# Weight splits of the mixer in halves, and two of the attention output's splits at the end of their slot

## The reference

```python
h = rms_norm(x, norm_mix_g); proj = h @ w_in
ca, cg, q, k, v, iq, ik, iw, z, xbc, dt = split(proj)
u = silu(layer_norm(causal_dwconv31(ca * sigmoid(cg))))      # group A
att = sparse_attention(rms_norm(q), rms_norm(k), v, iq, ik, iw, rel_bias)  # top 128 keys a query
y = ssd_scan(silu(causal_dwconv4(xbc)), softplus(dt + dt_bias), ...)       # Mamba-2, chunks of 128
y = rms_norm((y + d_skip * xs) * silu(z))
x = x + concat([u, att, y]) @ w_out
h = rms_norm(x, norm_ffn_g)
fa, fg = split(causal_dwconv3(h @ w_up))
x = x + (silu(fg) * fa) @ w_down
```

## Time and profile before

| | us |
|---|---|
| median of 3 runs | 713.55 (713.54 to 713.59) |
| profiled execution, its own time | 713.43 |
| span of that profile | 711.7 |
| busy: PE, DVE, ACT, POOL | 694.2, 547.5, 380.7, 140.5 |
| w_lo whole, DVE line 644 | 24 x 2.32, 7.9 idle before them |
| w_hi whole, ACT line 938 | 24 x 1.91, 3.6 idle before them |

### The profile page before, as it was taken

How to read it: one execution, slowest core, us unless ns; L and a number is a source line. 1 busy time by engine, 2 the same in 40 slices (tenths; PEclk the granted TensorE clock), 3 DMA queues, 4 the chain that set the end, 5 groups by cost and what they waited for, 6 DMA issues and landing times.

```text
span 711.7 us, 9787 instructions
## 1 busy us (share of the span) xinstructions
PE 694.2 (98%) x3402; PEld 558.0 (78%) x3402; DVE 547.5 (77%) x852; ACT 380.7 (53%) x570; POOL 140.5 (20%) x114
## 2 busy tenths in 40 slices
PE   4999999999999999999999999999999999999998
PEld 3776888767676788788898888888888888888886
DVE  4368979987899958677668687886766776997995
ACT  6354655989878775533463444344243333654660
POOL 2000477844465302233400000000000000000000
PEclk9999999999999999999999999999999999999999
DMA  8731314112121243312326578766688647864442
GB/s 247 225 138 61 119 59 119 60 60 83 36 62 58 62 177 104 103 60 61 89 90 175 182 205 250 217 170 188 183 244 250 188 154 293 294 221 146 164 163 88
DMA packets 87555, 104.10 MB, mean 146 GB/s; under 512 B 6872, under 2 KB 65592, under 8 KB 87520
## 3 DMA queue, kind: packets, MB, share of 16 engines
q1 hardware_dynamic: 87375, 103.12, 46.2%
q10 hardware_dynamic: 144, 0.52, 0.2%
...
## 4 chain that ended last, share of the span: by engine, by line
PE 79%; DVE 10%; ACT 6%; issue 2%; POOL 2%; DMA 1%; DVEq 0%; ACTq 0%; POOLq 0%
PE bank L1771 70%; DVE u_acc L626 3%; PE bank L1777 3%; DVE w_lo L644 2%; DVE xbcT L1431 2%; PE bank L1791 2%; ACT w_hi L938 1%; POOL u_acc L864 1%; PE bank L2035 1%; DVE prob L1410 1%; PE bank L1930 1%; DMA x_in<-in_x 1%; PE bank L1979 1%; ACT prob L1056 1%; PE bank L1955 1%
## 5 line engine op out<-in xcount | busy, mean ns | idle before, releaser
L1771 PE MATMUL bank<-h_hi,w_hi 128*128 128x512 f32 (+1 forms) x496 | 192.7, 389 | 0.0
L1771 PE MATMUL bank<-h_hi,w_lo 128*128 128x512 f32 (+1 forms) x496 | 189.9, 383 | 0.0
L1771 PE MATMUL bank<-h_lo,w_hi 128*128 128x512 f32 (+1 forms) x496 | 189.8, 383 | 0.0
L1625 DVE SCALAR_TENSOR_TENSOR f<-bank,prm,f 128x511 f32<-128x511 f32 x88 | 65.8, 747 | 60.9 <-ACT f L1186 55.4
L1771 PEld LDWEIGHTS bank<-h_hi,w_hi 128*128 128x128 f32 x496 | 93.3, 188 | 19.6 <-issue 2.1
L1771 PEld LDWEIGHTS bank<-h_hi,w_lo 128*128 128x128 f32 x496 | 93.2, 188 | 18.6
L1771 PEld LDWEIGHTS bank<-h_lo,w_hi 128*128 128x128 f32 x496 | 93.3, 188 | 17.4
L864 POOL TENSOR_TENSOR u_acc<-tapped,u_acc 128x511 f32<-128x511 f32 (+29 forms) x60 | 89.0, 1483 | 44.3 <-ACT tapped L1133 41.0
L1186 ACT ACTIVATE f<-bank,prm 128x512 f32<-128x512 f32 x44 | 34.2, 777 | 70.6 <-PE bank L1771 70.4
L644 DVE TENSOR_TENSOR w_lo<-w_raw,w_hi 128x2048 fp32r<-128x2048 f32 x24 | 55.7, 2320 | 8.0 <-ACT w_hi L938 7.9
L626 DVE SCALAR_TENSOR_TENSOR u_acc<-u_in,prm,u_acc 128x511 f32<-128x511 f32 (+29 forms) x60 | 53.3, 901 | 0.9
...
## 6 DMA issues: line engine op xcount, KB each, us to landing
...
```

What stands on the lines that cost most here:

```text
L1625: ins = dve.scalar_tensor_tensor(out=fbuf[:, 2 * s + v, i:], in0=bank[FFN_BANK[2 * s + v]][:, 0:SEQ - i], scalar=prm[:, bass.ds(tile + (R_ ...
L1771: ins = pe.matmul(o, a, b, start=first and i == 0 and q == 0, stop=last and i == n - 1 and q == 2)
```

## The change

It splits each mixer chunk's high and low part in two halves of 1024 columns. The first half of the high part stays in slot 4c - 4 and its second half goes to 4c - 3; the first half of the low part stays where the whole one was and the second goes to slot 4c - 2. Chunk 23 has all four in slot 4c - 4; chunk 18 has both low halves in 4c - 2. New semaphores `w_hi_half` and `w_lo_half` count first halves; `w_hi_ready` and `w_lo_ready` count second halves, so that PE, SP and the reuse of slots wait for the whole chunk as before. `attout` of blocks 1 and 2 moves from `front` to `fill`. Code for a share of the low part on POOL, which was unused (`POOL_LO` was empty), is removed. The order of instructions on PE, POOL and SP is the same as before.

```diff
@@ make_plan
     for c in range(1, UP0 + 1):
-        fill[4 * c - 4].append(("hi", c))
-        fill[4 * c - (2 if c == LATE_LO else 3 if c < UP0 else 4)].append(("lo", c))
+        one = 0 if c == UP0 else 1
+        fill[4 * c - 4].append(("hi", c, 0))
+        fill[4 * c - 4 + one].append(("hi", c, 1))
+        fill[4 * c - (2 if c == LATE_LO else 4 - one)].append(("lo", c, 0))
+        fill[4 * c - 4 + 2 * one].append(("lo", c, 1))
...
         if hp == NPAIR - 1:
-            front[n + 1].append(("attout", b))
+            (fill if b in (1, 2) else front)[n + 1].append(("attout", b))
@@ PLAN
-        ("norm", 3), ("hTev", 0), ("hTev", 1), ("hi", 0), ("hTev", 2), ("hTev", 3), ("hTlo", 0),
-        ("hTlo", 1), ("hTlo", 2), ("hTlo", 3), ("lo", 0), ("wsplit",)] + make_plan()
+        ("norm", 3), ("hTev", 0), ("hTev", 1), ("hi", 0, 0), ("hi", 0, 1), ("hTev", 2), ("hTev", 3), ("hTlo", 0),
+        ("hTlo", 1), ("hTlo", 2), ("hTlo", 3), ("lo", 0, 0), ("lo", 0, 1), ("wsplit",)] + make_plan()
@@ SP
-                if s[0] == "lo" and s[1] + NSLOT < UP0 + 2:
+                if s[0] == "lo" and s[2] == 1 and s[1] + NSLOT < UP0 + 2:
                     load(s[1] + NSLOT)
@@ ACT
-            def split_hi(c):
-                act.wait_ge(w_landed[c % NSLOT], 32 * (c // NSLOT + 1))
-                if c >= NSLOT:
-                    act.wait_ge(acc_step, STEP[("chunk", c - NSLOT)])
-                act.activation(whi[:, c % NSLOT, :], wraw[:, c % NSLOT, :], ACT.Copy)\
-                    .then_inc(w_hi_ready, 1)
+            def split_hi(c, n):
+                if n == 0:
+                    act.wait_ge(w_landed[c % NSLOT], 32 * (c // NSLOT + 1))
+                    if c >= NSLOT:
+                        act.wait_ge(acc_step, STEP[("chunk", c - NSLOT)])
+                act.activation(whi[:, c % NSLOT, half_cols(n)], wraw[:, c % NSLOT, half_cols(n)], ACT.Copy)\
+                    .then_inc(w_hi_ready if n else w_hi_half, 1)
@@ DVE
                 elif k == "lo":
-                    part_lo(dve, s[1], w_lo_ready)
+                    _, c, n = s
+                    dve.wait_ge(w_hi_ready if n else w_hi_half, c + 1)
+                    w = (slice(None), c % NSLOT, half_cols(n))
+                    dve.tensor_tensor(wlo[w], wraw[w], whi[w].bitcast(F32), ALU.subtract)\
+                        .then_inc(w_lo_ready if n else w_lo_half, 1)
```

More of the change, by code:

```diff
@@ L92 @@
 DW_POOL = (1, 2)
-POOL_COLS = 640
-POOL_LO = []
 def turn_banks(b):
@@ L636, in width, with half_cols @@
             return 2048 if p < NP2 else 1536
[L638 to L645 removed]
+        def half_cols(n):
+            return slice(1024 * n, 1024 * n + 1024)
         @block.sync
@@ L865, in _ @@
                                            u_acc[:, j, i:], ALU.add).then_inc(dw_taps[j], 1)
-                elif k == "lo" and s[1] in POOL_LO:
-                    part_lo(pool, s[1], pool_lo_ready)
                 elif k == "seg":
@@ L1004, in _ @@
                 elif k == "hi":
-                    split_hi(s[1])
+                    split_hi(*s[1:])
                 elif k == "idx":
```

15 lines of the change are left out of this document (1 added, 14 removed).

## The result

| | before | changed |
|---|---|---|
| median, us | 713.57 (713.54 to 713.63, 4 runs) | 728.06 (726.56 to 728.13, 4 runs) |
| profiled execution, its span | 713.43, 711.7 | 728.04, 726.2 |

The ratio is 1.0197, with a 95% interval of 1.0185 to 1.021. The change costs 14.5 us. The forecast was 719.2, and its range ended at 720.9.

What follows compares the result with a forecast made beforehand. TensorE, busy 98% of the span, was taken as the bound, with DVE full from 182 to 245 us. Terms 2.5 + 0 + 0 + 2.5 + 0.5 + 1.0 - 0.8 = 5.7 us gave 719.2, range 716.2 to 720.9.

Steps and rivals of the forecast that it cites:

- Extra cost of the halves: All 24 chunks: a pair costs ACT 0.1 us more and DVE 0.06, nearly all beside TensorE's work.
- Chunk 2: Chunk 2's first quarter: TensorE waits for the second half of w_lo until 48.65 us, +2.5 us, bounds 2.3 to 2.7.
- rival C: A wait at chunk 2 or near 230 us drops TensorE's clock to 1.2 GHz, costing 2.72 us: 722, chance 0.02.
- Chunks 7 to 9: TensorE 0.9 us late at chunk 7, absorbed in its wait at 135.29: 0, bounds -0.4 to 0.9.
- 135 to 182, and chunks 12 and 13: Stretch 135 to 182 us: 0, within -0.6 and +0.6; chunks 12 and 13, among the other chunks: 0.
- Block 2: Attention output of block 2: DVE stands 3.1 us for att_hi, unit 15's scores come 3.4 later; +2.5, upper bound 3.4.
- SSD: SSD steps: second half of w_hi between b_tok and ssm_hi costs +0.5, then +1.0; bounds together 0.3 to 1.9.
- x2n: Last chunk: DVE takes the first half 0.9 us earlier, shortening TensorE's wait at 358.08: -0.8, between -0.9 and 0.

Runs made afterwards that it cites:

- the cut kernel before: Kernel before with GpSimd's 58 convolution tap additions cut to one column each, all splits whole: 710.60 us.
- chunk 2 alone: Kernel before with only chunk 2 in halves, placed as in the changed kernel: 716.42 and 716.49 us, and 717.87, 717.88 and 717.91.
- the kernel with chunk 2 restored: Changed kernel with chunk 2's four steps back at their old places: 721.02, 723.79, 723.92 and 726.72 us.
- the cut kernels: Kernel before and changed kernel, both with GpSimd's tap additions cut to one column: 710.60 and 718.09 us, difference 7.5.

## Why the prediction was wrong

The direction, chunk 2, the cause and length of DVE's stand for att_hi, and the SSD steps were right. The size was not: 5.7 us against 14.5. Two steps failed: the price of a piece on DVE, and the clock, which was put at nothing in the sum.

- **Extra cost of the halves.** This is the step that failed first and cost most. It set 0.06 us of DVE for a pair, from two halves of the FFN's last pass, where GpSimd does nothing. In the mixer GpSimd adds taps, and DVE stands for them. DVE's time on w_lo went from 55.7 (24 x 2.32) to 64.2 us, of which 4.9 us are standing (from 60 to 300 us) and 3.6 are how two halves are shown, and its taps grew by 3.2 us. The rows of before already had the sign of it: w_lo of chunk 9 took 2.54 us and not 2.29, with its start at 129.52 inside a GpSimd addition:

```profile
128.54 1.38 POOL L864 TENSOR_TENSOR u_acc<-tapped,u_acc 128x495 f32<-128x495 f32 x1
```

- **Chunk 2.** 2.5 forecast, 2.48 measured. The 0.18 us by which TensorE is late before it aren't the halves': it is 0.17 late there in the cut kernel before, too, where all splits are whole. "Nothing between 46 and 135 us gives it back" holds.
- **The clock.** It stood as rival C with 0.02 and 2.7 us. It is 1.74 us behind chunk 2 in the profiled execution, and 1.43 in 3 of 5 runs of chunk 2 alone. It should have been a term of the sum: the longest wait that the earlier trace rows shows is 0.91 us, so those rows said nothing of a wait of 2.3. The fall near 230 us, which the rival named too, came and cost nothing.
- **Chunks 7 to 9.** The 0.9 at chunk 7 came, and was to vanish in the wait at 135.29. It does in the trace of the kernel with chunk 2 restored, where the halves of chunk 9 take 1.23 us each and 1.08 comes back. In the changed kernel they take 2.27 and 1.88, and TensorE falls back by 1.85 us more instead.
- **135 to 182, and chunks 12 and 13.** 0.40 at chunk 11 is within the bound of 0.6. The 0.92 and 0.35 at chunk 13 were taken as 0. There the second low half stands between a unit's scores and its reciprocal, and the three taps behind it took 4.64 us, and 3.04 before. With GpSimd cut, this loss is nil. DVE's rows of the changed kernel, and then of the kernel before:

```profile
202.94 1.35 DVE L1325 TENSOR_TENSOR w_lo<-w_raw,w_hi 128x1024 fp32r<-128x1024 f32 x1
204.21 4.64 DVE L627 SCALAR_TENSOR_TENSOR u_acc<-u_in,prm,u_acc 128x489 f32<-128x489 f32 x3
208.77 0.15 DVE L1413 RECIPROCAL stats<-stats 128x2 f32<-128x2 f32 x1
```
```profile
196.41 3.04 DVE L626 SCALAR_TENSOR_TENSOR u_acc<-u_in,prm,u_acc 128x489 f32<-128x489 f32 x3
199.37 0.16 DVE L1416 RECIPROCAL stats<-stats 128x2 f32<-128x2 f32 x1
```

- **Block 2.** 3.07 us of standing, as forecast, but the term was 5.0 and not 2.5, and beyond its upper bound of 3.4; that the clock was low for 1.59 of it changes nothing, as shown above. From the scores of unit 13 to those of unit 15 DVE falls back by 6.25 us (7.78 late, then 14.03), and 3.4 were forecast: the taps took 3.75 and 3.95 in place of 2.90 and 2.95, and a half took 1.97.
- **SSD.** 1.30 measured, 1.5 forecast. The 0.58 at dec came at TensorE's earlier wait, and the 0.94 at sct came in full both times.
- **x2n.** -0.8 forecast, 0.04 measured. The half did start earlier, and GpSimd took the lead away.

By place, 6.8 of the 8.8 us between forecast and result lie where DVE's rows show it standing for GpSimd (chunks 7 to 9 2.75, chunks 12 and 13 0.73, block 2 2.49, x2n 0.84), and 1.74 are the clock at chunk 2; chunk 11 with 0.40 and the SSD steps with -0.20 are the small ones. The 7.0 us that go with GpSimd's additions are about as much, but don't divide in this way: in the cut kernels block 2 costs 0.5 where 2.5 had been forecast, and the 0.9 of chunk 7 stays, since the cut kernel before gains as much at chunk 9. So the agreement of the two sums is in part luck. What isn't settled is how often each order of the two engines comes, and what decides it: the kernel with chunk 2 restored spreads over 5.7 us, and only one of its four runs has a trace.
